# Slot table by one-hot matmul, empty slots left out of gathers and stores, outputs stored by pair

## The reference

```python
g_logits = h @ w_grp + b_grp;  p_g, g_idx = top_k(softmax(g_logits), 1)      # 4 groups
e_logits = (h @ w_exp + b_exp) of group g_idx;  p_e, e_loc = top_k(softmax(e_logits), 2)
gate = p_g * p_e / sum(p_e);  expert = g_idx * 8 + e_loc
# rows sorted by expert, padded into blocks, one expert per block
y = (silu(xb @ w1[e]) * (xb @ w3[e])) @ w2[e]
out = zeros.at[row_tok].add(y * row_gate)
```

## Time and profile before

| | us |
|---|---|
| median of 3 runs (2648.88 to 2658.66) | 2651.09 |
| the profiled execution | 2651.05 |
| its span | 2649.2 |

### The profile page before, as it was taken

How to read it: one execution, slowest core, us unless ns; L and a number is a source line. 1 busy time by engine, 2 the same in 40 slices (tenths; PEclk the granted TensorE clock), 3 DMA queues, 4 the chain that set the end, 5 groups by cost and what they waited for, 6 DMA issues and landing times.

```text
span 2649.2 us, 32240 instructions
## 1 busy us (share of the span) xinstructions
PE 2199.2 (83%) x13486; PEld 1167.1 (44%) x13486; DVE 682.7 (26%) x1382; ACT 462.0 (17%) x1041; POOL 199.4 (8%) x267
## 2 busy tenths in 40 slices
PE   6899888859999597777777599999998688777773
PEld 3345788854644432222222344776455333222221
DVE  6204666772202310000000420541021210000003
ACT  3211444431111100000000100641021000000001
POOL 1000111111000110000000100000000200000001
PEclk9999899979999698888899799899999798988887
DMA  4023000011423479999998421002325399999995
GB/s 129 32 98 132 2 3 3 3 65 48 145 80 159 159 287 401 405 400 397 396 403 322 139 88 64 33 17 95 121 96 210 148 403 404 404 404 407 406 398 196
DMA packets 128519, 536.49 MB, mean 203 GB/s; under 512 B 19688, under 2 KB 29072, under 8 KB 112016
## 3 DMA queue, kind: packets, MB, share of 16 engines
q1 hardware_dynamic: 107648, 492.14, 47.5%
q0 software_dynamic: 10272, 25.75, 3.1%
q10 hardware_dynamic: 10480, 16.86, 1.9%
HBM read 503.22 MB, written 31.49 MB: 202 GB/s over the span
## 4 chain that ended last, share of the span: by engine, by line
PE 61%; DMA 24%; DVE 6%; issue 5%; SPq 2%; ACT 1%; POOL 1%; DVEq 0%; ACTq 0%; POOLq 0%
DMA big<-in_moe_w 23%; PE ps L1496 17%; PE ps L1483 10%; PE ps L1827 8%; PE ps L1602 6%; PE ps L1846 3%; PE ps L1542 2%; PE ps L1703 1%; SPq L452 1%; PE ps L1695 1%; PE ps L1469 1%; PE ps L1756 1%; PE ps L1768 1%; PE ps L1589 1%; PE ps L1717 1%
## 5 line engine op out<-in xcount | busy, mean ns | idle before, releaser
L1827 PE MATMUL ps<-big 128*64 128x512 f32 x2048 | 526.3, 673 | 178.8 <-DMA big<-in_moe_w 178.7
L1496 PE MATMUL ps<-big 128*128 128x512 f32 x1024 | 440.6, 592 | 0.0
L1827 PEld LDWEIGHTS ps<-big 128*64 128x64 f32 x2048 | 182.4, 154 | 519.7 <-issue 519.7
L1496 PEld LDWEIGHTS ps<-big 128*128 128x128 f32 x1024 | 194.3, 190 | 242.6 <-issue 242.5
L1483 PE MATMUL ps<-big 128*128 128x512 f32 (+1 forms) x768 | 277.9, 524 | 6.6 <-issue 6.6
L1413 DVE SCALAR_TENSOR_TENSOR big<-big,ps 128x256 f32<-128x256 f32 x64 | 26.9, 421 | 929.8 <-ACT big L941 929.8
L1846 PE MATMUL ps<-big 128*64 128x512 f32 x1024 | 237.2, 606 | 33.3 <-ACT big L948 33.3
L1483 PEld LDWEIGHTS ps<-big 128*128 128x128 f32 x768 | 146.3, 191 | 136.2 <-issue 128.9
L1602 PE MATMUL ps<-big 64*64 64x64 f32 x5632 | 179.5, 220 | 7.2 <-DVE big L1133 5.4
L1602 PEld LDWEIGHTS ps<-big 64*64 64x64 f32 x5632 | 172.4, 136 | 14.7 <-issue 8.8
L948 ACT ACTIVATE big<-ps 128x256 f32<-128x256 f32 x64 | 24.6, 384 | 718.3 <-PE ps L1836 715.9
(11 more groups left out here) (281 smaller groups left out, 1960.9 us busy)
## 6 DMA issues: line engine op xcount, KB each, us to landing
big<-in_moe_w SPq DMA_DIRECT2D x192, 2048.0 KB, 30.4
big<-in_mx_wkv SPq DMA_DIRECT2D x8, 2048.0 KB, 7.9
y_rows<-big ACTq DMA_DIRECT2D x128, 128.0 KB, 7.1
big<-in_rw_wrkv SPq DMA_DIRECT2D x6, 2048.0 KB, 8.5
big<-in_mb_wqkv SPq DMA_DIRECT2D x6, 2048.0 KB, 8.1
y_rows<-zero SPq DMA_DIRECT2D x2, 4096.0 KB, 24.5
big<-in_mx_wq SPq DMA_DIRECT2D x4, 2048.0 KB, 8.1
big<-in_mx_wo SPq DMA_DIRECT2D x4, 2048.0 KB, 8.2
```

Source lines behind the costliest of these rows:

```text
L1496: ins = mm(d[:], lhsT=lhs[:, k, t * P:(t + 1) * P], rhs=w[:, k, :], start=k == 0, stop=k == KT - 1)
L1827: ins = mm(ps[2 + b][half * BR:(half + 1) * BR, :], lhsT=hgT[b][:, k], rhs=w13[set_][:, :, k, half * 256:(half + 1) * 256], start=k == 0, ...
```

## The change

- The bank order gets a stage `table` behind `rank`. The 14 rank matmuls become 5 of 160 columns over a zero-padded `cnts`; the two one-hots lie in one tile `o12`, so that several DVE instructions become one of twice the size.
- DVE splits each pair's slot number into block and row and makes one-hot matrices of both, the block one times (pair number + 1). PE multiplies them (8 x 2 matmuls), which gives the table row x block of pair numbers in PSUM, in both partition halves. DVE makes index tables of it in SBUF: `idx_rows` for gathers, `idx_y` for stores, with an index beyond the bound where the slot is empty. The scatters, the table in DRAM, its zeroing and the index loads go.
- h_rows holds each token twice (row = pair number 2 x token + choice), so it is stored by two DMAs.
- Gathers take their indices from idx_rows with a bounds check that leaves out rows beyond the bound. The gather buffers are cleared by two POOL copies from `zero` at the start of each layer's routing, and lie elsewhere (one in `scratch`).
- Stores of y are indirect DMAs of POOL's (128 rows of 2 KB with the bounds check) into y_rows by pair number; ACT issues none. A prologue issues one all-empty store per buffer.
- At the end SP waits for the stores and loads each token tile with one plain DMA of 1 MB (four), since a token's two outputs lie side by side.

```diff
-NBP = NB + 1
+NBP = NB + 2
+PAD = 65536.0
...
+                sp.wait_ge(down_done[l], count)
+                for b in range(2):
+                    sp.wait_ge(y_stored[l][b], (count + (1 - b)) // 2 * 16 + 16)
+                for t in range(TT):
+                    sp.dma_start(combined[t], y_rows[l].rearrange("(t p k h) c -> t p (k h c)", t=TT, k=2, h=2)[t]
+                                 ).then_inc(combined_loaded[l][t], 16)
...
-                for k in range(2):
-                    for t in range(TT):
-                        if k == 0 and t == 0:
-                            pool.wait_ge(dest_ready, l + 1)
-                        pool.indirect_dma_start(
-                            slot_tok[l], bass.IndirectOffsetOnAxis(ap=dest_i[:, k, t:t + 1], axis=0),
-                            tok_i[:, t:t + 1], None).then_inc(ids_stored, 16)
-                pool.wait_ge(ids_stored, 16 * 8 * (l + 1))
...
+                wait_filled(pool, ("route", l))
+                for b in range(2):
+                    pool.tensor_copy(hg[b].rearrange("p (a c) -> p a c", c=256),
+                                     zero[0:BR].unsqueeze(1).to_broadcast([BR, C // 256, 256])).then_inc(rows_cleared, 1)
+                pool.wait_ge(rows_cleared, 2 * (l + 1))
+                pool.wait_ge(idx_ready, l + 1)
+                pool.wait_ge(rows_stored, 32 * (l + 1))
...
                     if n_block >= 2:
                         pool.wait_ge(rowsT[l], n_block - 1)
-                    pool.dma_start(idx[b][:], ids_of[n_block]).then_inc(ids_loaded[l][b], 16)
-                    pool.wait_ge(ids_loaded[l][b], 16 * (n_block // 2 + 1))
                     pool.indirect_dma_start(hg[b], None, h_rows[l],
-                                            bass.IndirectOffsetOnAxis(ap=idx[b][:], axis=0)
-                                            ).then_inc(gathered[l][b], 16)
+                                            bass.IndirectOffsetOnAxis(ap=idx_rows[0:BR, n_block:n_block + 1], axis=0),
+                                            bounds_check=2 * T - 1, oob_is_err=False).then_inc(gathered[l][b], 16)
+
+                def scatter(n_block):
+                    b = n_block % 2
+                    pool.wait_ge(y_out[l], n_block + 1 + PRE)
+                    pool.indirect_dma_start(y_rows[l],
+                                            bass.IndirectOffsetOnAxis(ap=idx_y[:, n_block:n_block + 1], axis=0),
+                                            y[b], None, bounds_check=4 * T - 1, oob_is_err=False
+                                            ).then_inc(y_stored[l][b], 16)
...
+                for n_block in range(E):
+                    if n_block + 4 <= E + 1:
+                        gather(n_block + 4)
+                    scatter(n_block)
...
+                link(V.tensor_tensor(picked, o12, bc(rank, [P, 2, TT, E], 1), ALU.mult))
+                link(V.tensor_reduce(dst2, picked, AX, ALU.add))
+
+                link(V.tensor_scalar(blk, dst2, -(BR - 1) / 2, 1 / BR, ALU.add, ALU.mult))
+                link(V.tensor_scalar(blk, blk, ROUND_MAGIC, None, ALU.add))
+                link(V.tensor_scalar(blk, blk, ROUND_MAGIC, None, ALU.subtract))
+                link(V.scalar_tensor_tensor(row, blk, -float(BR), dst2, ALU.mult, ALU.add))
...
+                link(V.tensor_tensor(blk1h, bc(iota_rows[:, 0:NBP], [P, 2 * TT, NBP], 1),
+                                     bc(pairs_of(blk), [P, 2 * TT, NBP], 2), ALU.is_equal))
+                V.tensor_tensor(row1h, bc(iota_rows, [P, 2 * TT, BR], 1), bc(pairs_of(row), [P, 2 * TT, BR], 2),
+                                ALU.is_equal)
+                V.tensor_tensor(blk1h, blk1h, bc(pairs_of(pair_no[:]), [P, 2 * TT, NBP], 2), ALU.mult
+                                ).then_inc(dest_ready, 1)
...
+                tab = bank(name)[:, 0:NBP]
+                link(V.tensor_scalar(pad_, tab, 0.5, PAD, ALU.is_lt, ALU.mult))
+                ins = V.scalar_tensor_tensor(idx_f, tab, -1.0, pad_, ALU.add, ALU.add)
+                empties(ins, name)
+                wait_emptied(dve, name)
+                V.tensor_copy(idx_rows, idx_f)
+                V.tensor_scalar(idx_y, idx_f, 2.0, pair_sel[:, 1:2], ALU.mult, ALU.add).then_inc(idx_ready, 1)
...
+                for j in range(TT + 1):
+                    ins = mm(d[:, 0:(TT + 1) * E], lhsT=before[:] if j == 0 else ones[:],
+                             rhs=cnts[:, (TT - j) * E:(2 * TT + 1 - j) * E], start=j == 0, stop=j == TT)
                 finish(ins)
+                pe.wait_ge(dest_ready, l + 1)
+                d = start(("table", l))
+                for i in range(2 * TT):
+                    for half in range(2):
+                        ins = mm(d[half * BR:(half + 1) * BR, 0:NBP], lhsT=row1h[:, i], rhs=blk1h[:, i], start=i == 0,
+                                 stop=i == 2 * TT - 1)
+                finish(ins)
...
-                pe.wait_ge(ids_stored, 16 * 8 * (l + 1))
                 keep_clock(10)
                 pe.wait_ge(gathered[l][0], 16)
```

More of the change, by code:

```diff
@@ L91, in bank_group_order @@
         o += [("xattn_out", l, half, t) for half in range(2) for t in range(TT)]
-        o += norm(n) + [("route", l), ("rank", l)]
+        o += norm(n) + [("route", l), ("rank", l), ("table", l)]
         n += 1
@@ L666, in _ @@
-                for first in range(E + 1, NBP, 5):
-                    with pool.If(count + 1 > first):
+                                            bass.IndirectOffsetOnAxis(ap=idx_rows[0:BR, n_block:n_block + 1], axis=0),
[7 more added lines that the diff above has]
+                                            ).then_inc(y_stored[l][b], 16)
@@ L668, in _ @@
+                pool.wait_ge(items_ready, l + 1)
+                count = pool.value_load(item_is[l][0:1, NX:NX + 1], min_val=0, max_val=NB)
+                for first in range(E + 2, NBP, 5):
+                    with pool.If(count + 2 > first):
                         gather(first)
+                        scatter(first - 2)
                         for n_block in range(first + 1, min(first + 5, NBP)):
-                            with pool.If(count + 1 > n_block):
+                            with pool.If(count + 2 > n_block):
@@ L1801, in _ @@
                 d = start(("rank", l))
-                for t in range(TT + 1):
-                    for j in range(min(t + 1, TT)):
-                        last = j == min(t, TT - 1)
-                        ins = mm(d[:, t * E:(t + 1) * E], lhsT=before[:] if j == t else ones[:], rhs=cnt[:, j],
-                                 start=j == 0, stop=last)
-                finish(ins)
-                wait_emptied(pe, ("rank", l))
+                for j in range(TT + 1):
+                    ins = mm(d[:, 0:(TT + 1) * E], lhsT=before[:] if j == 0 else ones[:],
+                             rhs=cnts[:, (TT - j) * E:(2 * TT + 1 - j) * E], start=j == 0, stop=j == TT)
+                finish(ins)
+                pe.wait_ge(dest_ready, l + 1)
[5 more added lines that the diff above has]
+                finish(ins)
+                wait_emptied(pe, ("table", l))
                 for name in ORDER[nxt[0] - 8:nxt[0]]:
```

139 lines of the change are left out of this document (58 added, 81 removed).

## The result

The changed kernel took 2585.02 us (median of 4 runs, 2574.62 to 2590.55) against 2652.07 us for the kernel before on the same chip: a ratio of 0.9739 (95% interval 0.9701 to 0.9778). The prediction said 2614 us, range 2586 to 2641. The direction was right; the gain was 67 us instead of 37, just outside the range.

What follows compares the result with a forecast made beforehand. The prediction took the expert stage to be bound by DMA transfers of weights, not PE. From 2651.1 us it took 9.2 for the start, 4.2 for the end and 24 for bytes: 2613.7, say 2614 us, range 2586 to 2641.

Steps and rivals of the forecast that it cites:

- Bytes in the stage: Expert stage: gathers and stores leave out empty slots, taken at 12 us a layer, 24 in all.
- dealing in fours: Stage transfers: partitions dealt to engines in fours; first engine spared 31% of a store, sum 8 us higher.
- full value: Expert stage: gain if all 16 engines share the halved gathers and stores, 24 us a layer.
- even relief: Rival for the expert stage: skipped rows are spread so all engines lose half, 2590 us; chance 28%.
- Start: Routing to first expert matmul: shorter by 4.8 us in the first layer, 4.4 in the second.
- port charge: Routing start: POOL's clearing copies hold up DVE ops with two SBUF inputs, charged at 2.0 us a layer.
- up to 3 more: Start: further gain in us if the clock-keeping matmuls find the clock already up; left out of the sum.
- What ends last at the start: Start: the clock-keeping matmuls, not the gather, end last, 3.4 us behind the gather.
- End: Each layer's combining after the last y copy: shorter by 2.0 us, second layer 2.2; bounds 0 and 6.
- Taken at nothing: Second copy of h, moved zeroing and new waits on POOL's queue: each priced at no time.
- No relief: Rival for the expert stage: skipped rows still sent or first engine gates entirely, 2638 us; chance 22%.
- Slower, a packet costs what it costs: Rival: software-queue packets cost the same whatever their size, skipped ones are sent, 2695 us; chance 12%.

Runs made afterwards that it cites:

- x2: Changed kernel with empty slots of gathers fetching row 0 again, stores still leaving empties out: 2622.57 us.
- x4: Changed kernel with nothing left out: gathers fetch row 0 for empty slots, stores write them to spare rows: 2632.91 us.
- x12: Changed kernel plus one plain load of 256 KB an item from ACT's queue into partitions 0 to 63: 2678.39 us.
- x9: Changed kernel with the filled slots of a block spread over all its 64 rows instead of from row 0 up: 2590.34 us.
- x3: Changed kernel with empty slots of stores written to spare rows, gathers still leaving empties out: 2600.76 us.
- x1: The changed kernel itself, unedited, timed again beside the other runs: 2581.40 us.
- x13: Changed kernel plus one plain load of 256 KB an item from ACT's queue, laid on 128 partitions of 2 KB: 2625.77 us.
- x14: Changed kernel with block rows gathered to partitions 0 to 31 and 64 to 95, transposes made selection matmuls: 2572.64 us.
- x17: x14 with the empty slots of gathers fetching row 0: 2584.79 us.
- x15: Changed kernel without the two POOL copies that clear the gather buffers: 2579.97 us.
- x16: x15 with most clock-keeping matmuls moved from behind the table to before it, while PE waits for DVE's slots: 2580.42 us.
- x10: Changed kernel plus one more gather an item with all 64 rows left out by the bounds check: 2590.15 us.
- x7: Changed kernel plus two gathers an item of 16 rows each, on partitions 0 to 15: 2706.81 us.
- x8: Changed kernel plus two gathers an item of 16 rows each, on every fourth of 64 partitions: 2678.90 us.
- x11: Changed kernel plus one more full gather an item, 64 rows of 4 KB: 2728.78 us.

## Why the prediction was wrong in size and right in kind

- **What bounds the kernel: right.** The stage is bound by the weights' transfers, bytes left out of it shorten it, and time taken out of the start comes off the end. x2 to x4 and x12 show the first, the table of stretches the second.
- **Bytes in the stage, the step that failed:** "But a weights transfer ends when its slowest engine has ended", and from it "I take the middle, 12 us a layer, 24 in all". The stages gained 23.0 and 21.3 us. The rate did not fall (406 GB/s at a busy share of 1.01), x9, which by the forecast's own dealing evens the engines out, won nothing, and in x12 all the lost time is in longer packets: nothing shows an engine that the others wait for. The Trainium skill's dealing in fours ("DMA: Bandwidth & Descriptors", section "The descriptor swizzle"), by which the sum was to be 8 us higher, is not shown wrong by this as a dealing, only as a price: no row tells which engine moved which row, and it would have put the time further off. Without this step the prediction's own full value, 24 us a layer, stands, and the sum becomes 2590, its rival "even relief", at 28%. That rival comes within 5 us partly by luck: its start is 8 us too small, its stages 4 and its ends 2 too large, and 4 us came in ahead of routing. I chose the middle between two ends without a row that showed gating; with the windows at a busy share of 1.02 it should have leaned to the even end.
- **Its full value was right for a partly wrong reason.** I had it from the packets' share of the engines' time (314 GB/s for the software queue), and by bytes 21.5 us. Gathers and stores do not cost alike: the stores' empties cost 19 us in all (I had 25), the gathers' 32 (x4 less x3) to 41 (x2 less x1), where I had 27.6 for half of both layers and x1's windows give their bytes 23. The low rate of that queue had another cause than tiny packets or its kind: x12 has it without either, 16.85 MB in 59 us, about 286 GB/s, where x13 has about 357. Its gathers are laid over partitions 0 to 63 alone (x12, x13, x14, x17).
- **Start: mis-sized by half.** Predicted -4.8 and -4.4, measured -8.6 and -8.9. The table matmuls were taken at 5.7 us and took 1.95: twice the nearest row, for the clock, on a row (0.089 us a piece) that was itself too dear; 32 instructions in 1.95 are 0.061 a piece. That is 3.7 us of each layer, and the largest part of the miss. The port charge of 2.0 us was 1.0 (0.27 + 0.77 beyond the undisturbed ops' 0.18; x15 gives 0.5 to 2.3). It was real, as the rule that the prediction cites from the Trainium skill ("SBUF — State Buffer", section "SBUF: two separate sides") has it: the two ops, each with two SBUF inputs, end at 901.79 and 902.77 us, 0.04 and 0.03 behind the two copies. But only two ops met the copies, the second for nearly its whole length, and half of the copies' 2.06 us cost nothing. The clock matmuls ran without a break between the ten and the four, 28 instructions in 7.78 and 9.19 us where the sum had 9.1 (7.12 for the ten and 1.99 for the four): of the "up to 3 more" that I had left out of it, 1.3 came in the first layer and nothing in the second. The other way went the rank matmuls (3.05 for 2.8) and small steps, 0.4 to 0.6 a layer, and in the first layer the router's matmuls, 1.8. With these, 4.8 and 4.4 become 8.4 and 8.7, against 8.6 and 8.9 measured.
- **What ends last at the start: right.** The chain runs through the clock matmuls and not through the gather. x16 takes this away, and the gather ends last.
- **End: right in its steps.** -1.1 and -1.4 for -2.0 and -2.2; the combining itself, from the last copy on, is 1.8 us shorter in the first layer. SP issued 4.4 us behind the last copy (4.7 forecast), the first MB was used 5.2 us later (4.9), and eight ops took 10.6 (10.4).
- **Taken at nothing: right.** The second copy of h costs nothing visible: DMA is at 0.05 from 912 to 935. POOL's queue delays no store: before its stores POOL sits idle 283.0 us in all for ACT's copies.
- **The rivals.** "No relief" is out (x4 against x1, 51.5 us). "Slower, a packet costs what it costs" is out: x10 sends 5120 more packets for 6 us, uncertain by 7, where 0.21 us each over 16 engines would be 67.

**Open.** Why a transfer over 64 partitions lengthens its own and the weights' packets: its half of SBUF, or how its rows are dealt to the engines (x14 speaks for more than the half). x7, x8 and x11 cost more than twice their bytes (125, 97 and 147 us for 8.4, 8.4 and 16.8 MB), and x11 costs 50 more than x12 with the same bytes into the same partitions. So a full software gather beside the weights is dearer than a plain load by another 24 us a stage. Of these 50 us, 44 are again the weights' packets (49.5% of 2728.0 us against 48.8% of 2676.4); why, no run here tells. In x7, x8 and x11 POOL also waits for an earlier added gather before it goes on; x10 has x11's waits and costs next to nothing, but its gathers have little to land, so what such a wait costs behind full ones was not tested. The sum of x2 and x3 (60) and x4 (51.5) differ by about their uncertainty. How much of x14's relief PE holds back was argued only.

## What to carry to other kernels

Where a stage is bound by DMA, price a transfer by its bytes, and ask whether it is laid over all 128 partitions: one over partitions 0 to 63 cost double here (x12, x13). Laying the gathers over 128 partitions was worth as much as leaving their empty rows out: x17, which fetches them all, took 2584.79 us, the kernel after 2585.02. Rows skipped by a bounds check are nearly free, so masking beats fetching padding. Don't halve a gain for a suspected imbalance that no row shows: look at the rate and the busy share of the full windows first, and try the even dealing as an experiment.

## What the runs showed of the hardware that was not expected

- 256 KB an item written by one transfer to partitions 0 to 63 cost 97 us over 64 items, the same bytes on 128 partitions 44; the stream fell to 384 GB/s in one and stayed at 406 in the other, with the engines' busy share at 1.02 in both. The difference lies in longer packets, 41 of the 53 us in the weights' own.
- With the kernel's own gathers laid over 128 partitions instead of 64 the stream rose from 407 to 416 (x14) and to 420 GB/s (x17), although in x14 nine filled rows in ten still went to partitions 0 to 31.
- An indirect transfer whose rows are all beyond the bound adds packets (5120 for 64 transfers of 64 rows and their completions) but hardly any bytes or time.
- 32 matmul instructions of 49 columns on 64 output partitions took 1.95 us behind an idle stretch of 6.5 us, and 1.14 us (x16, x18) where clock-keeping matmuls ran in that stretch.
- POOL's 1.03 us copy of 64x1024 stretched a DVE op on 128x16 elements from 0.18 to 0.95 us, almost the length of the copy.
